# Gate, up and down projections of a gated ConvFFN as seven block products over token halves, in two stages with the hidden tiles in DRAM

## What is computed

```python
def causal_dwconv(x, buf, w, b):            # width 3, along the tokens
    xp = jnp.concatenate([buf.astype(x.dtype), x], axis=1)
    y = b
    for j in range(width):
        y = y + w[j] * xp[:, j:j + t]
    return y, xp[:, xp.shape[1] - (width - 1):]

def conv_ffn(xn, buf, w_g, w_u, w_c, b_c, w_d):
    g = xn @ w_g
    gc, new_buf = causal_dwconv(g, buf, w_c, b_c)
    return (jax.nn.gelu(gc) * (xn @ w_u)) @ w_d, new_buf
```

## Time and profile before

| | us |
|---|---|
| median of three runs | 2642.78 |
| lowest, highest | 2642.22, 2642.88 |
| span of the profiled execution | 2640.3 |
| PE busy in it | 2589.7 |
| DVE, POOL, ACT busy | 1606.4, 1133.4, 867.6 |

### The profile page before, as it was taken

How to read it: one execution, slowest core, us unless ns; L and a number is a source line. 1 busy time by engine, 2 the same in 40 slices (tenths; PEclk the granted TensorE clock), 3 DMA queues, 4 the chain that set the end, 5 groups by cost and what they waited for, 6 DMA issues and landing times.

```text
span 2640.3 us, 42777 instructions
## 1 busy us (share of the span) xinstructions
PE 2589.7 (98%) x16013; PEld 2419.6 (92%) x16013; DVE 1606.4 (61%) x2183; ACT 867.6 (33%) x1229; POOL 1133.4 (43%) x919
## 2 busy tenths in 40 slices
PE   8999998899999999999999999999999999999999
PEld 7878886699999999999999999999999999999998
DVE  6456566533666666666676544524666677766674
ACT  5575666532222222222222524423222222222221
POOL 3233333224544454444555411344555555544541
PEclk9999999999999999999999999999999999999999
DMA  5101107731111111111111211211111111111112
GB/s 178 55 28 44 43 25 261 270 114 46 59 41 48 48 48 48 48 42 46 48 48 33 62 36 39 62 40 59 54 41 47 48 48 48 48 42 45 48 32 72
DMA packets 208445, 164.11 MB, mean 62 GB/s; under 512 B 9901, under 2 KB 182038, under 8 KB 208334
## 3 DMA queue, kind: packets, MB, share of 16 engines
q1 hardware_dynamic: 207278, 160.35, 19.5%
q10 hardware_dynamic: 576, 2.10, 0.2%
q0 software_dynamic: 480, 0.11, 0.0%
HBM read 147.83 MB, written 14.69 MB: 62 GB/s over the span
## 4 chain that ended last, share of the span: by engine, by line
PE 78%; DVE 0%; ACT 0%; issue 0%; DVEq 0%
PE psum_all L148 50%; PE psum_all L2011 16%; PE psum_all L2485 6%; PE psum_all L2025 2%; PE psum_all L1999 1%; PE psum_all L2001 1%; PE psum_all L2537 0%; PE psum_all L2501 0%; PE psum_all L2525 0%; PE psum_all L2355 0%; PE psum_all L2571 0%; PE psum_all L1679 0%; DVE mixed_odd L2696 0%; ACT operand_hi_a L1784 0%; PE psum_all L2542 0%
## 5 line engine op out<-in xcount | busy, mean ns | idle before, releaser
L108 POOL TENSOR_TENSOR w_lo_part<-w_raw,w_hi_part 128x1024 fp32r<-128x1024 f32 x94 | 227.4, 2419 | 578.1 <-ACT w_hi_part L104 578.1
L2243 DVE TENSOR_TENSOR x_residual<-x_residual,psum_all 128x512 f32<-128x512 f32 (+1 forms) x616 | 449.7, 760 | 19.6
L148 PE MATMUL psum_all<-operand_hi_c,w_hi_part 128*128 128x364 f32 (+1 forms) x1344 | 297.5, 330 | 0.6 <-DVE operand_lo_c L1788 0.6
L148 PE MATMUL psum_all<-operand_hi_a,w_hi_part 128*128 128x364 f32 (+1 forms) x1344 | 297.7, 330 | 0.2 <-DVE operand_lo_a L1788 0.2
L148 PE MATMUL psum_all<-operand_hi_c,w_lo_part 128*128 128x364 f32 (+1 forms) x1344 | 295.5, 328 | 0.0
L148 PE MATMUL psum_all<-operand_lo_a,w_hi_part 128*128 128x364 f32 (+1 forms) x1344 | 295.3, 328 | 0.0
L148 PE MATMUL psum_all<-operand_hi_a,w_lo_part 128*128 128x364 f32 (+1 forms) x1344 | 295.2, 328 | 0.0
L148 PE MATMUL psum_all<-operand_lo_c,w_hi_part 128*128 128x364 f32 (+1 forms) x1344 | 294.9, 327 | 0.0
L113 POOL TENSOR_TENSOR w_lo_part<-w_raw,w_hi_part 128x1024 fp32r<-128x1024 f32 x54 | 130.6, 2419 | 372.3 <-ACT w_hi_part L97 372.2
L2227 DVE TENSOR_TENSOR gate_conv_ffn<-psum_all,gate_conv_ffn 128x1092 f32<-128x1092 f32 x48 | 62.2, 1295 | 347.7 <-PE psum_all L148 347.7
L2011 PE MATMUL psum_all<-hidden_hi_ffn,w_down_hi_ffn 128*128 128x512 f32 x616 | 240.7, 391 | 0.0
(11 more groups left out here) (354 smaller groups left out, 5031.6 us busy)
## 6 DMA issues: line engine op xcount, KB each, us to landing
w_raw<-in_w_gate_dram SPq DMA_DIRECT2D x48, 512.0 KB, 3.8
w_raw<-in_w_up_dram SPq DMA_DIRECT2D x48, 512.0 KB, 3.8
w_down_raw_ffn<-in_w_down_dram SPq DMA_DIRECT2D x44, 512.0 KB, 4.0
pages<-in_cache_k_dram SPq DMA_DIRECT2D x64, 256.0 KB, 3.5
pages<-in_cache_v_dram SPq DMA_DIRECT2D x64, 256.0 KB, 5.4
w_raw<-in_w_in_even_dram SPq DMA_DIRECT2D x20, 512.0 KB, 4.0
w_raw<-in_w_in_odd_dram SPq DMA_DIRECT2D x16, 512.0 KB, 4.8
x_spill<-x_residual SPq DMA_DIRECT2D x8, 546.0 KB, 5.3
```

The source lines that it names most:

```text
L108: pool.tensor_tensor(lo, self.raw[:, raw, :], hi.bitcast(F32), ALU.subtract).then_inc(self.s_lo, 1)
L148: mm = pe.matmul(bank[:, c, 0:width(c)], w, x[:, chunk(c)], start=(k == 0 and step == 0), stop=(k == last and step == 2))
L2243: dve.tensor_tensor(dst, dst, src, op).then_inc(self.pair_read, 1)
```

## The change

The FFN is rewritten as two stages, written out without a loop, and `dense` is left only for the output projections of the mixers.

**Stage 1** (24 jobs, gate and up in turn, two hidden tiles each). The operand is normalised x in seven blocks over the two halves of the tokens (544 each) and the two halves of the input tiles: four blocks of x and sums of them, made once in the opening. One job is seven products of 4 input tiles x 3 split products x 2 chunks of 272 columns = 24 matmuls. The products go to three PSUM groups `d`, `a`, `bb` of two banks; `a` and `bb` are added to after their first product has been read. Weights come as one transfer of 1 MB per job; POOL makes four sums of 512 columns and seven low parts of 512, ACT seven high parts. ACT copies four results out of PSUM, DVE adds three onto them. Only then does DVE multiply the gate by the rms scale, as an instruction of its own over SBUF, and convolve; it multiplies up by gate (`hidden_tile`) and forms four sums of half tiles (`hidden_sum`). The seven hidden blocks of a pair are stored to DRAM. The residual x is stored to DRAM before, and its SBUF is used for gate, up and raw weights.

**Stage 2** (16 jobs: four rounds of three pairs of hidden tiles, four quarters each). The blocks come back from DRAM (`piece`, 3 x 544 columns) and are split; one job is seven products of 3 x 3 x 2 matmuls of 272 columns, added by DVE onto the reloaded residual (`add_residual`). In the last job of a round DVE and POOL also make the low parts of the next round's pieces (1632 columns each).

The core of the diff. Of what is removed only the lines that carry the counts are shown:

```diff
-    PRODUCTS = ((0, 0, 0, True, 0), (4, 1, 1, True, 0), (2, 2, 2, True, 0), (5, 3, 0, False, 1), (7, 4, 1, False, 2),
-                (3, 5, 2, True, 3), (6, 6, 0, False, 4))
...
-            for j, (op, x, bank, first, reads) in enumerate(self.PRODUCTS):
-                if p == 0:
-                    pe.wait_ge(self.t_lo, 8 * t + 2 + j)
-                if reads:
-                    pe.wait_ge(self.pair_read, 7 * s + 1 + reads)
-                col = slice((op % 4) * P, (op % 4 + 1) * P)
-                w_hi, w_lo = (self.blocks(d, p, op // 4)[:, col] for d in (b.d_hi, b.d_lo))
-                for step, (wt, xt) in enumerate(((w_hi, b.t_hi), (w_lo, b.t_hi), (w_hi, b.t_lo))):
-                    mm = pe.matmul(core.ps[:, base + bank, :], wt, xt[:, x, :], start=first and step == 0, stop=step == 2,
-                                   skip_group_check=True)
-                mm.then_inc(self.product, 1)
...
+HALF = USED // 2
+HB = HALF // 2
+PAIRS = FT // 2
+JOBS1 = 2 * PAIRS
+ROUNDS, QUARTERS = 4, 4
+JOBS2 = ROUNDS * QUARTERS
+JOBS = JOBS1 + JOBS2
+B21, B11, T1, T2, B22, NT4, T3 = range(7)
...
+    GROUPS = (("d", True), ("a", True), ("bb", True), ("a", False), ("bb", False), ("d", True), ("a", False))
...
+    def block_sums(self, pool, n, first, second):
+        if first:
+            pool.wait_ge(self.w_in[n % 2], 16 * (n // 2 + 1))
+            if n:
+                pool.wait_ge(self.w_lo, 7 * n)
+            pool.tensor_tensor(self.sums(n, "S1"), self.part(n, 0, 1), self.part(n, 1, 1), ALU.add
+                               ).then_inc(self.w_sum, 1)
+            pool.tensor_tensor(self.sums(n, "S3"), self.part(n, 0, 0), self.part(n, 0, 1), ALU.subtract
+                               ).then_inc(self.w_sum, 1)
+        if second == "S2":
+            pool.wait_ge(self.w_sum, 4 * n + 1)
+            pool.tensor_tensor(self.sums(n, "S2"), self.sums(n, "S1"), self.part(n, 0, 0), ALU.subtract
+                               ).then_inc(self.w_sum, 1)
+        if second == "S4":
+            pool.wait_ge(self.w_sum, 4 * n + 3)
+            pool.tensor_tensor(self.sums(n, "S4"), self.part(n, 1, 0), self.sums(n, "S2"), ALU.subtract
+                               ).then_inc(self.w_sum, 1)
+    def block_lo(self, pool, n, i):
+        pool.wait_ge(self.w_hi, self.done(n, i))
+        if i not in (0, 1, 5):
+            pool.wait_ge(self.w_sum, 4 * n + (0, 0, 1, 3, 4, 0, 2)[i])
+        pool.tensor_tensor(self.block(n, i, 1).rearrange("p (q c) -> p q c", c=P), self.source(n, i),
+                           self.block(n, i, 0).bitcast(F32).rearrange("p (q c) -> p q c", c=P), ALU.subtract
+                           ).then_inc(self.w_lo, 1)
+    def gate_scale(self, pool, t, r):
+        pool.wait_ge(self.gelu_ready, 2 * t + r + 1)
+        pool.tensor_tensor(self.conv[:, r, :], self.conv[:, r, :], self.core.rb[:, 0:USED], ALU.mult
+                           ).then_inc(self.gr_ready, 1)
...
+    def multiply(self, pe, n, i, ready=None):
+        name, first = self.GROUPS[i]
+        b = self.banks[name]
+        depth = self.depth(n)
+        x_hi, x_lo = self.operand(n, i, 0), self.operand(n, i, 1)
+        w_hi, w_lo = self.block(n, i, 0), self.block(n, i, 1)
+        order = [(q, s) for s in range(3) for q in range(depth)]
+        if ready:
+            order = [(q, s) for q in range(depth) for s in range(3)]
+        mm = None
+        for at, (q, s) in enumerate(order):
+            if ready and s == 0:
+                ready(q)
+            wt, xt = ((w_hi, x_hi), (w_lo, x_hi), (w_hi, x_lo))[s]
+            for h in range(2):
+                mm = pe.matmul(self.core.ps[:, b + h, 0:HB], wt[:, q * P:(q + 1) * P], xt[:, q, HB * h:HB * (h + 1)],
+                               start=first and at == 0, stop=at == len(order) - 1, skip_group_check=True)
+        mm.then_inc(self.product, 1)
...
+    def tensor(self, pe, behind=None):
+        self.opening(pe)
+        for n in range(1, JOBS):
+            m = n - JOBS1
+            dve = 3 * n if n < JOBS1 else 3 * JOBS1 + 7 * m
+            for i in range(7):
+                pe.wait_ge(self.w_lo, 7 * n + i + 1)
+                if n < JOBS1:
+                    if i == 0:
+                        pe.wait_ge(self.act_out, 4 * n)
+                    elif i == 1:
+                        pe.wait_ge(self.dve_out, dve)
+                    elif i == 3:
+                        pe.wait_ge(self.dve_out, dve + 1)
+                    elif i == 4:
+                        pe.wait_ge(self.act_out, 4 * n + 2)
+                    elif i == 6:
+                        pe.wait_ge(self.act_out, 4 * n + 3)
+                else:
+                    if i == 0 and m == 0:
+                        pe.wait_ge(self.act_out, 4 * JOBS1)
+                    elif i in (0, 1):
+                        pe.wait_ge(self.dve_out, dve - 1 + i)
+                    elif i in (3, 4, 6):
+                        pe.wait_ge(self.dve_out, dve + (0, 0, 0, 2, 3, 0, 4)[i])
+                    if m % QUARTERS == 0:
+                        pe.wait_ge(*self.x_lo_done(m // QUARTERS, i))
+                self.multiply(pe, n, i)
+                if m == 1 and i == 0:
+                    self.turn_state_rows(pe)
+                if behind and m >= JOBS2 - QUARTERS:
...
+            last = t == PAIRS - 1
+            if t:
+                for i in (1, 4, 6):
+                    self.add_out(dve, 2 * t, i)
+            self.conv_part(dve, o, t, 0)
+            self.add_out(dve, 2 * t + 1, 1)
+            self.conv_rest(dve, o, t, 0)
+            self.conv_part(dve, o, t, 1)
+            self.conv_rest(dve, o, t, 1)
+            self.add_out(dve, 2 * t + 1, 4)
+            if last:
+                self.piece_lo(dve, 0, B21)
+                self.piece_lo(dve, 0, B11)
+            self.hidden_tile(dve, t, 0)
+            self.hidden_sum(dve, t, T1)
+            self.add_out(dve, 2 * t + 1, 6)
+            if not last:
+                self.hidden_tile(dve, t, 1)
+                for i in (T3, T2, NT4):
+                    self.hidden_sum(dve, t, i)
...
+    def add_out(self, dve, n, i):
+        dve.wait_ge(self.product, self.done(n, i))
+        dve.wait_ge(self.act_out, 4 * n + {1: 1, 4: 3, 6: 4}[i])
+        if i == 6:
+            dst = self.target(n, 1).rearrange("p (c h n) -> p c h n", c=2, h=2)
+            src = self.group("a").unsqueeze(1).to_broadcast((P, 2, 2, HB))
+        else:
+            dst = self.half(self.target(n, 0), i == 4).rearrange("p (h n) -> p h n", h=2)
+            src = self.group("a" if i == 1 else "bb")
+        dve.tensor_tensor(dst, dst, src, ALU.add).then_inc(self.dve_out, 1)
...
+    def conv_part(self, dve, o, t, r):
+        f, par = 2 * t + r, self.params.par
+        gb, gc, xs = self.g[:, r, :], self.conv[:, r, :], self.mem.xs[:, r]
+        def tap(j):
+            return par[:, f + FT * j:f + FT * j + 1]
+        dve.wait_ge(self.dve_out, 6 * t + 2 + r)
+        g = gb[:, 2:2 + USED]
+        o.did(dve.tensor_tensor(g, g, self.core.rb[:, 0:USED], ALU.mult))
+        o.did(dve.tensor_copy(xs[:, :, 0:2], self.params.state[:, f, :].rearrange("p (s j) -> p s j", j=2)))
+        o.after()
+        if t:
+            dve.wait_ge(self.hc, 16 * t)
+        o.did(dve.tensor_scalar(gc, g, tap(2), tap(3), ALU.mult, ALU.add))
+        o.did(dve.tensor_copy(xs[:, :, 2:2 + SLEN], gb[:, 2 + SEQ:2 + USED].rearrange("p (s t) -> p s t", t=SLEN)))
+        o.after()
+        o.did(dve.scalar_tensor_tensor(gc, gb[:, 1:1 + USED], tap(1), gc, ALU.mult, ALU.add))
```

1306 lines of the change are left out of this document (708 added, 598 removed).

## The result

| | before | after |
|---|---|---|
| median of 4 runs, us | 2642.59 | 2893.28 |
| lowest to highest | 2642.22 to 2642.88 | 2889.75 to 2894.02 |
| span of the profiled execution | 2640.3 | 2891.4 |

The ratio is 1.0949, its 95% interval 1.0933 to 1.0964: slower by 251 us, where +246 had been forecast.

A forecast was written before the change was run, and what follows sets the result against it. PE alone was taken to bound both FFNs: 2640.3 - 117 (PE work) + 293 (pairs) + 70 (smaller terms) = 2886, with 2.5 around the span 2889 us. Main case 2790 to 2950; stated range 2600 to 2960.

The forecast's parts named there:

- PE work, -117 us: Both FFNs: fewer multiplications in gate and up save PE 58.5 us a layer, -117 for both (-105 to -129).
- both lines: Two estimates for a 272-column matmul: 128.6 ns from 363 and 512 columns, 126.5 from 256 and 363; 127.5 taken.
- The weight load: PE's weight loads stay hidden at 272 columns; rival that they show, 166 ns a matmul: about 3000 us, chance 0.02.
- DVE and POOL one for one: When both read SBUF only, each waits for the other's whole instruction, in turn, through an exclusive lock on shared ports.
- A pair at 55.0 us: Stage 1, walked operation by operation: a gate and up pair takes 55.0 instead of 42.8 us, +293 in all.
- The clock costs nothing: PE's slow clock after the 8 us wait is covered by the 2.5 us wait behind it; uncovered 41 us.
- Opening 15 us: Start of each FFN: making seven operands on DVE and POOL costs 15 us a layer, bounds 8 to 22.
- Entry 8 and turns 12: Stage 2, per layer: 8 us at entry (4 to 12), three turns of rounds at 4 each (2 to 6).
- Odd layer: nothing: The odd layer and the end cost nothing: same work, with enough done before its first product.
- the small terms: Opening, entry to stage 2 and turns of rounds: 35 us a layer, +70 for both.
- "Absorbed" at 2598: Rival: the DVE chain's waits are absorbed, 1.5 us a pair and half the smaller terms, 2598 us, faster; chance 0.20.
- its own opposite argument: Against absorbed waits: before, POOL was half busy and DVE had 4 to 10 us spare before each addition; now not.

The follow-up runs named there:

- a: Changed kernel with POOL's operations in jobs 2 to 23 of both first stages cut to 2 of each 128 columns, computation incomplete: 2619.2 us.
- b: Changed kernel with the POOL operations of jobs 2 to 23 of both first stages replaced by full-width fills that read nothing, computation incomplete: 2622.7 us.
- g: Changed kernel with 64 transposes into an unused bank before the wait for product 1 of every gate job from job 2 on: 2905.6 us.
- j: Changed kernel with POOL's sums and low parts in the opening's block work and the second stage replaced by fills, computation incomplete: 2792.7 us.
- c: Changed kernel with the convolution's scalar operations and sample copies moved from DVE to ACT: 2774.2 us.
- d: As c, with gate times rms moved from POOL to DVE and the up job's last addition before the hidden tile: 2959.5 us.
- e: As d, with the four weight sums of each up job made by DVE during the gate job instead of by POOL: 2829.7 us.
- i: Changed kernel with DVE's three T2 sums of the opening moved behind its addition for the last output tile: 2889.9 us.
- k: As d, with DVE's PSUM additions reordered: first ones moved ahead, hidden tile and T1 again before the up job's last addition: 2698.5 us.
- l: As k, with the four weight sums of each up job made by DVE, behind the gate job's first addition: 2697.8 us.
- m: Changed kernel with only DVE's order moved: up job's last and next gate job's first PSUM additions ahead of hidden tiles and sums: 2773.1 us.
- n: As l, with DVE's order changed again for pair additions, opening T2 sums and low parts at turns of rounds: 2584.7 us.

## Why the prediction was right, and where its sum was not

- **PE work, -117 us: mis-sized, measured -151.** A matmul of 272 columns took 125.0 ns, below both lines (126.5 and 128.6; by the prediction's own prices they give 126.9 and 128.5). The step that failed is the taking over of prices from 256, 363 and 512 columns: 2.5 ns x 12,096 is 30 us. The price at 256 columns was read off a row rounded to 0.12 us; from 701 to 1394 us these matmuls are 118.8 ns apart, and with 0.41 ns a column that gives 125.4 at 272, an estimate from rows before. The other 4 us a layer are in the sum for before, 829.6 where the FFN takes 833.6 with its small matmuls. The weight load was hidden, as said.
- **DVE and POOL one for one: right.** L2442's two elements take 1.31 us; runs a and b take the wait away with POOL's work. L2428's and L2420's mean were forecast near 2.3 and are 1.98 and 2.03 over jobs 1 to 23: 2.31 and 1.99 to 2.39 beside POOL, but 1.35 for L2428 once POOL has nothing to do. L2421's was forecast near 1.3 and is 1.60.
- **A pair at 55.0 us: measured 53.8.** The walk had 1.65 lost before product 3 (1.53 measured), 8.0 before product 1 (7.37) and 2.5 before the next product 3 (2.5 of slow clock, in run g 2.2 of waiting). Twelve pairs were counted at full price; the stretch of 23 jobs lost 134.6 where 146 stood, 269 in place of 293 for both. The waits that the walk ended in held within 0.7 us each. (Of the prediction's own range, 14 a pair gives 2932, not 2950.)
- **The clock costs nothing: right in a pair,** shown by run g for the spell behind the wait of 7.4, with one detail missed: the spell does not lie beside the wait of 2.5, it replaces it.
- **Opening 15 us: 24.5 measured,** above the upper bound of 22. The step that failed is that bound, which left out the clock: waits are 18.3 of the 24.5, slow clock the rest. Run j puts 13 of it on POOL's operations; in what is left there PE waits 6.4 us for DVE and 1.6 for ACT.
- **Entry 8 and turns 12, together 20: 40.2 measured.** A turn's waits were about right, 0.5 to 0.8 and then 3.7 us, against 4, but all three were followed by a slow clock (90 matmuls in 14.2, 14.3 and 13.0 us in place of 11.4). The entry was missed by half: waits of 4.3, 6.9, 0.5 and 1.2 us, and after each of the first two 18 matmuls in 4.4 us in place of 2.4. Of the 20 us missed, 14 are slow clock and 6 waits, nearly all at the entry. The step that failed is the one that let the clock cost nothing: it holds in a pair, where a wait lies behind the spell, and was taken over to places that have none. "Odd layer: nothing" cost 3.2.
- **Sum.** By these: -151 + 269 + 136 = 254, forecast -117 + 293 + 70 = 246. The gain was 34 us larger than forecast, the pairs lost 24 less and the small terms 66 more. The mechanism was right; that the total came within 4 us is luck, by cancelling.
- **Rivals.** "Absorbed" at 2598 was given 0.20, and its own opposite argument decided: turns are one for one. What I had not seen is how cheap it is to get there. DVE even ends with more work over SBUF (18.5 us a pair in place of 16.9). What it takes is additions ahead of what PE does not wait for, and ACT, idle for 63% of the time, for small operations.

The other forecasts of time, in us:

```
run   forecast         rival              measured
a     2630 to 2645     2880 to 2895       2619.2   faster than forecast
b     2630 to 2645     2880 to 2895       2622.7   faster than forecast
c     2640 to 2710     2845; 2750-2850    2774.2   missed
d     2650 to 2710     2780 or more       2959.5   the rival
e     2620 to 2665     2700 or more       2829.7   missed; in the rival's range, not its cause
g     2883 to 2903     2840 to 2856       2905.6   missed by 3, on the side away from the rival
i     2889 to 2897     2883 or less       2889.9   as forecast
j     2827 to 2843     2870 or more       2792.7   faster than forecast
k     2640 to 2710     2780 or more       2698.5   as forecast
l     2620 to 2660     2665 to 2720       2697.8   the rival
m     2763 to 2795     2840 to 2893       2773.1   as forecast
n     2570 to 2610     2640 to 2670       2584.7   as forecast
```

What stays open: why the clock falls after one wait of 2.6 us and not after the next.

## What to carry to other kernels

When two engines take turns on a resource, add up both engines' time over it for one period and hold it against the bounding engine's. In the nine kernels above no pair is more than 1 us shorter than the larger of the two, and where the sum is the smaller one, order was what was missing (e and l against n). In an in-order queue, put the operation the bounding engine waits for ahead of all that it doesn't, and look for idle time in front of the queue's late stretch: d was idle for 5.3 us and then late by 8.8. Count tiny operations too: the copy of 16 columns takes 1.60 us on average in the changed kernel and 0.17 without POOL's work. No run moved the tiny ones alone, so what that is worth by itself is not shown.

## What the hardware showed that I had not expected

- Matmuls of 272 columns follow each other at 125.0 ns in the run without waits and at 125.3 in the second stage, those of 256 at 118.8: from 256 to 272 the slope is that between 363 and 512 columns (0.4 ns a column), but a line drawn from 363 down misses both.
- POOL's fills don't hold up DVE's two-input operations (0.53 us inside one of 1.35), but a 16-column copy waits for one (0.53 in place of 0.17).
- The length of a wait alone doesn't decide whether the clock falls. In the changed kernel's first FFN none of ten waits of 1.5 to 1.8 us was followed by the lower level, and all of 7.2 us and more were. In run l 96 matmuls take 12.24 us after a wait of 2.56, at a granted clock of 1.00, and 13.84 after one of 2.65, with granted clocks of 0.88, 0.50 and 0.76 in the first three stretches of 2 us.
